# Two loops of TensorE products per contraction tile merged into one, in a two-block transformer kernel on one Trainium2 core

## The reference, cut to what matters

```
D_MODEL = 1024; SEQ = 256; DEPTH = 2; D_FF = 2816

def swiglu(h, w_gate_up, w_down):                 # block one, twice per layer
    a, b = jnp.split(h @ w_gate_up, 2, axis=-1)
    return (jax.nn.silu(a) * b) @ w_down

def conv_glu_ffn(x, w_up, conv_w, conv_b, w_down):  # block two, once per layer
    h = x @ w_up
    hp = jnp.pad(h, ((0, 0), (1, 1), (0, 0)))
    h = hp[:, :-2] * conv_w[0] + hp[:, 1:-1] * conv_w[1] + hp[:, 2:] * conv_w[2] + conv_b
    a, b = jnp.split(h, 2, axis=-1)
    return (jax.nn.gelu(a) * b) @ w_down
```

## Time and profile before

| what | value |
|---|---|
| median of three runs | 1955.67 us |
| lowest and highest | 1955.28 and 1956.16 us |
| profiled execution, its time | 1955.28 us |
| profiled execution, its span | 1953.5 us |
| PE (products) busy | 1941.9 us, 99% |
| PEld (weight loads) busy | 1659.3 us, 85% |
| DVE, ACT, POOL busy | 1363.0, 1035.2, 165.0 us |
| DMA, mean | 187 GB/s |
| granted TensorE clock | 1.00 of full speed |

### The profile page before, as it was taken

One profiled execution on the slowest core, in us unless ns is written; L12 is line 12 of the kernel. 1 busy time (PEld: TensorE's weight loads), 2 busy tenths in 40 slices (PEclk: granted clock), 3 DMA queues, 4 the chain that ended last, 5 costly groups with the idle time before them and its releaser, 6 DMA issues.

```text
span 1953.5 us, 27601 instructions
## 1 busy us (share of the span) xinstructions
PE 1941.9 (99%) x10534; PEld 1659.3 (85%) x10534; DVE 1363.0 (70%) x1652; ACT 1035.2 (53%) x1201; POOL 165.0 (8%) x152
## 2 busy tenths in 40 slices
PE   9999999999999999999999999999999999999998
PEld 8888978888888889788888978888888978888887
DVE  7666577666676666677666556577888666677887
ACT  6444555544454454655445554356556554456664
POOL 0000130000000003104002201040001301000000
PEclk9999999999999999999999999999999999999999
DMA  8555635455455546446555553564554554555552
GB/s 328 193 185 181 204 141 194 174 192 193 172 194 193 193 161 206 154 178 235 185 191 189 172 177 142 206 248 175 193 193 146 193 179 160 207 206 191 187 191 87
DMA packets 55132, 365.74 MB, mean 187 GB/s; under 512 B 6672, under 2 KB 7952, under 8 KB 12176
## 3 DMA queue, kind: packets, MB, share of 16 engines
q1 hardware_dynamic: 49680, 349.99, 50.1%
q0 software_dynamic: 1472, 9.44, 1.3%
q10 hardware_dynamic: 3904, 5.25, 1.0%
HBM read 359.40 MB, written 1.05 MB: 185 GB/s over the span
## 4 chain that ended last, share of the span: by engine, by line
PE 96%; DVE 1%; ACT 1%; issue 0%; DMA 0%; SPq 0%; ACTq 0%; DVEq 0%
PE gate_two L1694 12%; PE up_two L1694 12%; PE bank L1624 9%; PE bank L1626 9%; PE bank L1625 9%; PE gate_two L1624 8%; PE gate_two L1626 8%; PE gate_two L1625 8%; PE gate_two L1698 6%; PE up_two L1698 6%; PE bank L1837 1%; PE up_two L1868 1%; PE up_two L1852 1%; PE bank L2129 1%; ACT w_hi L569 0%
## 5 line engine op out<-in xcount | busy, mean ns | idle before, releaser
L1019 DVE TENSOR_TENSOR w_lo<-raw,w_hi 128x2048 fp32r<-128x2048 f32 x318 | 734.6, 2311 | 247.0 <-ACT w_hi L569 241.6
L569 ACT ACTIVATE w_hi<-raw 128x2048 fp32r<-128x2048 f32 x322 | 614.2, 1908 | 95.3 <-PE bank L1626 65.5
L1694 PE MATMUL gate_two<-br_parts,w_hi 128*128 128x512 f32 x1056 | 332.1, 396 | 0.4 <-DVE area L1076 0.2
L1694 PE MATMUL up_two<-br_parts,w_hi 128*128 128x512 f32 x1024 | 321.6, 395 | 0.0
L1698 PEld LDWEIGHTS gate_two<-br_parts,w_lo 128*128 128x128 f32 x1056 | 198.4, 188 | 46.2
L1698 PEld LDWEIGHTS up_two<-br_parts,w_lo 128*128 128x128 f32 x1024 | 192.4, 188 | 45.5
L1698 PE MATMUL gate_two<-br_parts,w_lo 128*128 128x256 f32 x1056 | 207.5, 278 | 0.0
L1698 PE MATMUL up_two<-br_parts,w_lo 128*128 128x256 f32 x1024 | 201.2, 278 | 0.0
L1624 PE MATMUL bank<-w_lo,hid_hi 128*128 128x512 f32 x480 | 187.1, 390 | 0.0
L1625 PE MATMUL bank<-w_hi,hid_lo 128*128 128x512 f32 x480 | 187.0, 390 | 0.0
L1626 PE MATMUL bank<-w_hi,hid_hi 128*128 128x512 f32 x480 | 186.7, 389 | 0.0
(11 more groups left out here) (274 smaller groups left out, 2961.6 us busy)
## 6 DMA issues: line engine op xcount, KB each, us to landing
raw<-stream SPq DMA_DIRECT2D x328, 1024.0 KB, 4.8
area<-rpb POOLq DMA_DIRECT2D x2, 1536.0 KB, 7.8
area<-rows POOLq DMA_DIRECT2D x3, 1024.0 KB, 5.1
raw<-stream SPq DMA_DIRECT2D x8, 256.0 KB, 7.7
softT<-area ACTq DMA_DIRECT2D x32, 64.0 KB, 5.3
area<-rows POOLq DMA_DIRECT2D x2, 768.0 KB, 4.7
konst<-consts SPq DMA_DIRECT2D x1, 1344.0 KB, 9.1
area<-xT ACTq DMA_DIRECT2D x4, 256.0 KB, 6.8
```

Of the source, the lines that this page charges most:

```text
L569: act.activation(w_hi[:, s, :], raw[:, s, :], ACT.Copy).then_inc(hi_ready[s], 1)
L1019: dve.tensor_tensor(w_lo[:, s, :], raw[:, s, :], w_hi[:, s, :].bitcast(F32), ALU.subtract).then_inc(lo_ready[s], 1)
L1694: pe.matmul(pair[:, f, :, :], w_hi[:, s, at:at + P], parts[:, :, k, :], start=k == 0, stop=False, skip_group_check=True)
```

## The change

In `halves`, the head of the second loop over `f` and the repeated computation of `at` go. The short product of a feature group is thus issued right behind the long product of the same group. The products, their operands, shapes, places in PSUM and flags are the same, and so is the last product, which raises `w_used`.

```diff
@@ def halves(c, pair, parts, k_first=lambda k: None) @@
                     at = k * 2 * P + f * P
                     pe.matmul(pair[:, f, :, :], w_hi[:, s, at:at + P], parts[:, :, k, :], start=k == 0, stop=False,
                               skip_group_check=True)
-                for f in range(2):
-                    at = k * 2 * P + f * P
                     e = pe.matmul(pair[:, f, 0, :], w_lo[:, s, at:at + P], parts[:, 0, k, :], start=False,
                                   stop=k == DT - 1, skip_group_check=True)
             return e.then_inc(w_used[s], 1)
```

## The result

The changed kernel takes 1967.34 us (median of five runs, 1966.80 to 1968.06) against 1955.67 us before (1954.98 to 1956.68): the ratio is 1.0058, with a 95% interval from 1.0046 to 1.0069. It is slower, by 11.7 us. Forecast were 1957 us in a range of 1947 to 1967. The profiled execution's span grew by nearly as much, from 1953.5 to 1964.8 us.

The account below looks back on a forecast made before the run. The prediction took the distances between TensorE product starts to bound the kernel. The profiled 1955.28 us plus 1 us for the added trips gave 1956.3, 1956.7 on the median's footing, stated as 1957 us, range 1947 to 1967 us.

Parts of the forecast that it names:

- What bounds the kernel: TensorE's distances between product starts set the time: products fill 1941.9 us of a 1953.5 us span.
- Nothing is added or moved beyond the neighbours: In `halves`, instructions, shapes, load count and waits stay the same; only each product's neighbours change.
- PSUM at nothing: A short product following the long one into the same PSUM bank costs nothing; upper bound within +16 us.
- The sum: Whole kernel: profiled 1955.28 us plus 1 us gives 1956.3, or 1956.7 on the median's footing, stated as 1957 us.
- its one term: Tile steps of `halves`: two long-to-short-and-back trips instead of one, about 1 ns each; +1 us over 1040 steps.
- The base line: A tile step of `halves`: two long products at 0.227 us and two short at 0.120 make 0.694 us.
- No load gets better cover by the exchange: In `halves`, a step has two loads under long and two under short products, before and after the change.
- The slower one: In `halves`, long products behind short ones run slow: 0.703 to 0.710 us a step, 1964 to 1972 us; chance 0.28.
- The faster rival: In `halves`, alternating cover keeps long products at 0.225 us, short at 0.115: 0.680 a step, 1940 us; chance 0.17.

Follow-up runs that it names:

- alt_banks: Changed kernel with each short product in the other PSUM bank than its long neighbours (long f=0 with short f=1 eight times, then the reverse): 1973.41 us.
- pair_rev: Kernel before, two long then two short products, but with the two short ones in reverse order (f=1, then f=0): 1955.32 us, ratio 1.0002.
- alt_load64: Changed kernel with 64 stationary columns instead of 128 in the long product from the second tile on: 1942.99 us.
- alt_448: Changed kernel with a short product of 448 columns instead of 256: 2137.92 us.
- alt_512: Changed kernel with a short product of 512 columns instead of 256, so all products are equally long: 2172.97 us.
- alt_both64: Changed kernel with 64 stationary columns instead of 128 in both long and short products from the second tile on: 1940.82 us.
- equal_load64: Changed kernel with short products of 512 columns too, and 64 stationary columns in the product on w_hi from the second tile on: 2190.93 us.
- pair_load64: Kernel before, its order kept, with 64 stationary columns instead of 128 in the long products from the second tile on: 1957.05 us.
- group_all: Kernel before with all 16 long products of a chunk first, then its 16 short ones: 1958.19 us, ratio 1.0015.

## Why the prediction was wrong

**What bounds the kernel: right.** PE's distances set the time, no wait came, the one that went was 0.2 us, and the added time is all PE's.

**Nothing is added or moved beyond the neighbours: right.** Waits, loads, other engines and the release of slots are as before. That the loads start with the product ahead of them was right too.

**PSUM at nothing: right.** alt_banks and pair_rev show it.

**The sum: wrong, by its one term.** The step that failed is "A trip from long to short and back thus adds about 1 ns to what the products take among their like". Two trips a step instead of one were to give 0.696 us. Measured are 0.706 us a step (two times 0.353): +10 ns and not +1, some 9 to 10 us over 1040 steps. The down chunks add the rest. The term had two faults. The base line, 0.694 us from runs of their like, is no floor, since the run of short ones has its own excess of 7 ns each (120 against the 113 of alt_load64). And the excess is not a sum over trips. Against a floor of 16 x 0.340 = 5.44 us an up chunk has 0.21 us of excess in the one-by-one order (16 trips), 0.13 in twos (8 trips), 0.17 in fours (4 trips) and 0.13 in one piece (1 trip): 13, 17, 43 and 130 ns a trip. Against the prediction's own base line (16 x 0.347 = 5.55 us) it is no single price either: 6, 3, 15 and about 15 ns. A count of trips thus said little, and a difference of two almost equal averages, taken from rows written to 10 ns, was read as a price. The chunk that it was read from also holds a fast first step (38.82 to 39.51, 0.69 us); in the records its settled steps take 0.697 us, which would have made the term 3 ns, still a third of what came.

**"No load gets better cover by the exchange": right as a count, wrong as an argument.** Cover is not what decides: alt_448 has full cover and the excess.

**What was left out: the neighbours' chunk.** The prediction held that down chunks stay at 5.45 us. They take 5.50, because the first products behind the alternating ones still run at 0.24 us. In the records the down chunks account for 2.9 us, more than all of the 2.6 us net outside `halves`.

**The rivals.** The slower one came true in size: it named 0.703 to 0.710 us a step and 1964 to 1972 us, with long products at 0.235. Measured: 232, 241 and 236 ns in turn for the long ones, 236 on average, short ones at 117, 1967.3 us. Its sign in the trace, the two long products at 0.46 to 0.47 us behind short ones and 0.45 behind long ones, was the one fact about history in the rows, and it should have carried the forecast: after the change every long product stands behind a short one. Its explanation, that short products use something up which long ones make good, is only in part borne out: alt_load64 shows that it is not the short product as such. The faster rival's step of 0.680 us exists, as alt_load64's, but only with a narrower load. The range ended 0.3 us below the result.

**What stays open.** The excess of the changed order is shown to hang on the order of lengths together with the widths of the products and their loads: it goes away with equal lengths at full width (alt_512) and with halved widths at unequal lengths (alt_load64, alt_both64). It is shown not to come from waits, banks or reading in stretches, the turn between the two weight buffers costs nothing at equal lengths, and a load that outlasts its product is not needed for it. Whether a narrower load or the narrower product that goes with it is what matters was not separated. How lengths and loads together give 353, 347 or 340 ns, why four by four is worse than two by two, and why narrowing harms in equal_load64 and pair_load64, no run here settles.

## What to carry to other kernels

In this kernel's dense stream of TensorE products, each with its own load, the order of long and short ones was worth some tenths of a per cent even where counts, loads and banks stayed the same: one-by-one alternation was the worst order tried per chunk (5.64 and 5.65 us), one long run of each kind the best (5.54 and 5.57). In between, fewer changes were not always better, as fours (5.59 and 5.61) did worse than twos (5.56 and 5.57). Look in the trace at the first products behind a change of length; if they stand further apart than those in a run, then an order that puts every product there can pay this each time, and an average over the old order does not show it. When grouping, leave chunks alone whose inputs arrive piece by piece, since the products moved back were filling waits there.

## What the runs showed of the hardware

After a run of short products the long ones need about five products to settle: in group_all, behind 16 short ones, their distances are 233, 236, 228, 232, 231 and then 227 ns; behind a down chunk they are 227 from the first. Behind the one-by-one order of the changed kernel, the down chunk's products need ten (241, 237, 233, 236, 224, 231, 236, 228, 232, 231, then 227), behind the two-and-two order only two (232, 231, then 227). In group_all the first short product behind long ones has 113 or 114 ns, the second 119, all others 120.

In `halves`, a load of 128 columns lasts 187 to 192 ns, of 96 columns 161 and of 64 columns 133 to 138, yet a product may start some 110 ns after its load has started: the load begins 2 to 5 ns behind the start of the product ahead, and the next product can follow that start by 113 ns. In no kernel did a load for a product of the full array (128 x 128) start ahead of the product before its own, so of the window of loads that the Trainium skill describes ("TensorE: Matmul & The Clock Gate", "Step-by-step: what each phase is for") one load ahead is all that these traces show for such products. It is otherwise at attention's products of half the array (64 x 128 on L1837 and 128 x 64 on L1868 of the kernel before), which start in pairs some 6 ns apart: there 160 loads start ahead of the product before their own, by up to 210 ns. The shortest distances that were kept up from product to product were 227 ns at 512 columns and 113 at 256. "Back-to-back issue gap" on the same page of the Trainium skill gives 216 and 109 for products alone, which no product of `halves` reached; single ones came to 224 and 112. Halving the width of A and its load gained 13 ns for a long and a short product in turn (alt_load64 against after) and cost 10 ns for two long ones in turn (equal_load64 against alt_512, 463 against 453).
